# Routing of a two-layer PEER trunk: index of head 0 first, four early gathers behind it, half 6 of the query weights split by VectorE

## What is computed

```python
q = (xt @ w_q).reshape(n_tok, PEER_HEADS, 2, D_QHALF)          # 8 heads, two halves of 128 each
sc = einsum("thcd,hckd->thck", q, sub_keys)                    # scores against 128 keys per half
top_s, top_i = top_k(sc, 16)                                   # "keys"
cand_s = top_s[:, :, 0, :, None] + top_s[:, :, 1, None, :]
best_s, best_j = top_k(cand_s, 16)                             # "pairs"
experts = take_along_axis(top_i0 * 128 + top_i1, best_j)       # "part": the index
gates = softmax(best_s)
h = einsum("thkd,td->thk", u_tab[experts], x)                  # 128 rows of 8 KB per token
out = einsum("thk,thkd->td", gates * gelu(h), v_tab[experts])
```

## Time and profile before

| | |
|---|---|
| median of 3 executions | 3293.93 us (3290.31 to 3294.55) |
| profiled execution: its time | 3297.1 us |
| profiled execution: span from first to last instruction | 3295.4 us |
| mean granted TensorE clock | 0.943 of 2.4 GHz |
| query product of layer 0 | 358.9 to about 461.2 us |
| query product of layer 1 | about 2043 to 2146 us |
| first ring dots (`first_dots`) of layer 0, layer 1 | 466.4 us, 2150.6 us |

### The profile page before, as it was taken

How to read it: one execution, slowest core, us unless ns; L and a number is a source line. 1 busy time by engine, 2 the same in 40 slices (tenths; PEclk the granted TensorE clock), 3 DMA queues, 4 the chain that set the end, 5 groups by cost and what they waited for, 6 DMA issues and landing times.

```text
span 3295.4 us, 44606 instructions
## 1 busy us (share of the span) xinstructions
PE 2879.7 (87%) x15107; PEld 2210.8 (67%) x15107; DVE 2466.0 (75%) x3641; ACT 825.6 (25%) x1274; POOL 1557.6 (47%) x1313
## 2 busy tenths in 40 slices
PE   9999987667777899999899999977768777999998
PEld 8887887666777644444697977966667776444443
DVE  6996698999999766666533555898899988766666
ACT  1014432113433500000233534422224335200000
POOL 0000567767677644444200002777676777544443
PEclk9999998888988999999999999988789889999999
DMA  8434499999999899999765334799999999999998
GB/s 259 153 128 153 150 362 422 421 421 412 419 417 421 309 410 406 409 409 402 267 211 179 129 138 156 258 409 421 422 422 416 416 419 353 376 410 405 409 407 344
DMA packets 293996, 1108.20 MB, mean 336 GB/s; under 512 B 22068, under 2 KB 120948, under 8 KB 220788
## 3 DMA queue, kind: packets, MB, share of 16 engines
q0 software_dynamic: 147456, 805.37, 60.3%
q1 hardware_dynamic: 146420, 301.26, 25.3%
HBM read 1104.45 MB, written 2.10 MB: 336 GB/s over the span
## 4 chain that ended last, share of the span: by engine, by line
DMA 39%; PE 27%; DVE 15%; issue 9%; POOL 7%; ACT 2%; SPq 0%; POOLq 0%; DVEq 0%; ACTq 0%
DMA ring<-in_peer_u,index_now 17%; DMA work<-in_peer_v,index_add 13%; PE ps L865 6%; DMA more_add<-in_peer_v,index_add 6%; PE ps L762 5%; DVE ring L1870 5%; POOL ring L604 5%; PE ps L805 5%; DVE ps L1942 3%; PE ps L816 2%; DMA work<-in_peer_v,index_v 2%; PE ps L944 1%; PE ps L1048 1%; DMA ring<-in_peer_w_q 1%; PE ps L1026 1%
## 5 line engine op out<-in xcount | busy, mean ns | idle before, releaser
L604 POOL DMA_INDIRECT ring<-in_peer_u,index_now x480 | 793.0, 1652 | 343.9 <-issue 137.9
L1870 DVE SCALAR_TENSOR_TENSOR ring<-ring,x_tok 128x2048 f32<-128x2048 f32 x372 | 843.4, 2289 | 102.8 <-DMA ring<-in_peer_u,index_now 101.5
L1101 PE MATMUL ps<-all_v,mix 128*128 128x512 f32 x1984 | 851.8, 592 | 0.0
L1101 PEld LDWEIGHTS ps<-all_v,mix 128*128 128x128 f32 x1984 | 377.0, 190 | 474.5 <-issue 474.5
L1054 PE MATMUL ps<-x_dot,work 128*128 128x128 f32 x3968 | 524.9, 296 | 113.3 <-DVE ps L1877 73.1
L1942 DVE SCALAR_TENSOR_TENSOR ps<-work,coef,ps 128x1024 f32<-128x1024 f32 x326 | 419.0, 1288 | 244.9 <-DMA work<-in_peer_v,index_add 202.6
L1054 PEld LDWEIGHTS ps<-x_dot,work 128*128 128x128 f32 x3968 | 502.4, 209 | 142.9 <-ACT work L1404 72.2
L588 POOL TENSOR_TENSOR w_lo<-ring,w_hi 128x512 fp32r<-128x512 f32 x104 | 134.0, 1324 | 829.2 <-ACT w_hi L1234 804.9
L1404 ACT ACTIVATE work<-ps 128x1024 f32<-128x1024 f32 x248 | 243.6, 1022 | 611.2 <-PE ps L1048 610.7
L1632 DVE TENSOR_TENSOR w_lo<-ring,w_hi 128x2048 fp32r<-128x2048 f32 x85 | 194.8, 2292 | 246.9 <-ACT w_hi L1234 246.8
L714 POOL DMA_INDIRECT work<-in_peer_v,index_add x256 | 242.0, 945 | 268.2 <-DVE ps L1942 220.5
(11 more groups left out here) (234 smaller groups left out, 3811.9 us busy)
## 6 DMA issues: line engine op xcount, KB each, us to landing
all_v<-in_peer_v SPq DMA_DIRECT2D x248, 512.0 KB, 6.8
ring<-in_peer_w_q SPq DMA_DIRECT2D x16, 2048.0 KB, 9.4
ring<-in_attn_w_kv SPq DMA_DIRECT2D x16, 2048.0 KB, 8.7
ring<-in_conv_w_in SPq DMA_DIRECT2D x14, 2048.0 KB, 9.0
ring<-in_conv_w_out SPq DMA_DIRECT2D x8, 2048.0 KB, 7.4
ring<-in_attn_w_q SPq DMA_DIRECT2D x8, 2048.0 KB, 8.2
ring<-in_attn_w_o SPq DMA_DIRECT2D x8, 2048.0 KB, 7.3
ring<-in_peer_u,index_now POOLq DMA_INDIRECT x480, 13.7
```

The costliest lines, as they stand in the source:

```text
L604: pool.indirect_dma_start(tile, None, u_tab, bass.IndirectOffsetOnAxis(ap=index_now[:, half, s:s + 1], axis=0)).then_inc(landed_in, 16)
L1101: mm = pe.matmul(ps[:, dense_bank(tb, q), :], mix[tb][:, row, :], tile[:, q * 512 - HALF:(q + 1) * 512 - HALF], start=False, stop=True, sk ...
L1870: dve.scalar_tensor_tensor(out=tile, in0=tile, scalar=1.0, in1=x_tok[:, tb, :], op0=ALU.mult, op1=ALU.mult, accum_out=coef[:, tb, slot]).t ...
```

## The change

The same operations on the same data are done in another order, with four differences of substance.
1. The index is made for head 0 alone (a part of 1 head), then for heads 1 to 3 together (3 heads). Before, heads 0 and 1 were indexed together, and then heads 2 and 3. The third part (heads 4 to 7) stays.
2. GpSimd splits halves 0 to 5, issues e0 to e3 in one go, and then splits half 7. VectorE splits half 6. From half 8 on they take turns as before. The gathers e4, e5 and e6, e7 stand at other places between the halves.
3. VectorE's dots of early tiles stand as 3, 3 and 2 between other work (2, 1, 2, 2 and 1 before); `route_keys` of token block 1 moves behind the keys and pairs of heads 4 and 5.
4. ScalarE places x into PSUM after half 2 instead of after half 1.

```diff
-                for u in range(8):
+                for u in range(6):
                     split_half(U_WQ[layer] + u)
                 pool.wait_ge(route[layer], part_done(0, 0))
-                gather_early(0, 3)
+                gather_early(0, ROOMS)
+                next_half(7)
+                gather_early(ROOMS, ROOMS + 1)
                 next_half(9)
-                gather_early(3, 5)
+                gather_early(ROOMS + 1, ROOMS + 3)
                 next_half(11)
-                gather_early(5, 7)
+                gather_early(ROOMS + 3, EARLY)
                 next_half(13)
-                gather_early(7, EARLY)
...
                 gather_first(4, U_RING)
+                pool.wait_ge(route[layer], part_done(0, 1))
                 for group in (2, 3):
...
-                for tb, first, group, pairs in ((0, 2, 4, 2), (0, 4, 8, 4), (1, 0, 0, 4), (1, 4, 8, 4)):
+                for tb, first, group, pairs in ((0, 1, 4, 2), (0, 4, 8, 4), (1, 0, 0, 4), (1, 4, 8, 4)):
...
                     if m == 1:
                         take_keys()
+                    if m == 2:
                         act.wait_ge(sk_taken, 4 * (layer + 1))
...
-                for h in range(2):
-                    route_keys(layer, 0, h, h + 1)
-                    route_pairs(layer, 0, h, h + 1)
-                part_numbers(layer, 0, 0, 2)
+                route_keys(layer, 0, 0, 1)
+                route_pairs(layer, 0, 0, 1)
+                part_numbers(layer, 0, 0, 1)
                 for c in range(2):
-                    part_key(layer, 0, 0, 2, c)
-                part_index(layer, 0, 0, 2)
+                    part_key(layer, 0, 0, 1, c)
+                part_index(layer, 0, 0, 1)
+                route_keys(layer, 0, 1, 2)
+                next_half(6)
+                route_pairs(layer, 0, 1, 2)
+                early_dots(0, 3)
                 next_half(8)
-                route_keys(layer, 1, 0, 2)
-                early_dots(0, 2)
+                early_dots(3, 6)
+                route_keys(layer, 0, 2, 4)
                 next_half(10)
-                route_keys(layer, 0, 2, 4)
-                early_dots(2, 3)
+                early_dots(6, EARLY)
                 route_pairs(layer, 0, 2, 4)
                 next_half(12)
-                early_dots(3, 5)
+                part_numbers(layer, 0, 1, 4)
+                for c in range(2):
+                    part_key(layer, 0, 1, 4, c)
+                part_index(layer, 0, 1, 4)
+                next_half(14)
                 route_keys(layer, 0, 4, 6)
-                next_half(14)
-                early_dots(5, 7)
                 route_pairs(layer, 0, 4, 6)
-                early_dots(7, EARLY)
-                part_numbers(layer, 0, 2, 4)
-                for c in range(2):
-                    part_key(layer, 0, 2, 4, c)
-                part_index(layer, 0, 2, 4)
+                route_keys(layer, 1, 0, 2)
                 first_dots(0, U_RING // 2)
```

More of the change, by code:

```diff
@@ L47 @@
 LN_HEAD = 9
-ROUTING = (("keys", 0, 0, 1), ("pairs", 0, 0, 1), ("keys", 0, 1, 2), ("pairs", 0, 1, 2), ("part", 0, 0, 2),
-           ("keys", 1, 0, 2), ("keys", 0, 2, 4), ("pairs", 0, 2, 4), ("keys", 0, 4, 6), ("pairs", 0, 4, 6), ("part", 0, 2, 4),
+ROUTING = (("keys", 0, 0, 1), ("pairs", 0, 0, 1), ("part", 0, 0, 1), ("keys", 0, 1, 2), ("pairs", 0, 1, 2),
+           ("keys", 0, 2, 4), ("pairs", 0, 2, 4), ("part", 0, 1, 4), ("keys", 0, 4, 6), ("pairs", 0, 4, 6), ("keys", 1, 0, 2),
            ("keys", 0, 6, 8), ("pairs", 0, 6, 8), ("logits", 0, 0, 8), ("part", 0, 4, 8), ("gate", 0, 0, 8),
```

## The result

The changed kernel takes 3343.55 us (median of 4, 3342.79 to 3344.54) against 3293.01 us of the kernel before: ratio 1.0157, interval 1.0145 to 1.0170. It is 50.5 us slower. The forecast was slower, 3328 us, with a range up to 3338: the direction was right and the size was too small, by 15.5 us. The profiled execution took 3344.5 us with a span of 3342.8 us.

A forecast was written before the change was run, and what follows sets the result against it. TensorE paces the query product and DMA bytes bound the dot phase behind it. Two TensorE stalls per layer delay the ring dots 17 us, twice 17 = 34 us on 3293.9 gives 3328 us; range 3308 to 3338.

The forecast's parts named there:

- The pace of the product and the bound behind it: TensorE paces the query product, waiting about 0.6 us in 13; the dot phase behind is bound by bytes at 422 GB/s.
- Step 1: Half 9 is rounded at 409.03 us as before, split by GpSimd from 411.50 to 416.5; e5's gather issues at 416.68.
- The weighing of the two queues: Gather beside a panel: half of 422 GB/s gives 7 us to landing; the measured row, 8.7 us, was used instead.
- Steps 2 and 3: e5 lands after 8.7 us at 425.4; VectorE idles some 9 us, splits half 10 at 435.2; TensorE stalls 7.3 us.
- Steps 4 and 5: e7 lands at 448.9, half 12 is split at 456.7; TensorE stalls 9.0 us, the product is 15.8 us late.
- Step 6: VectorE's three-head part takes 11 us ahead of half 14, split at 469.9; the product ends 16.5 us later.
- Step 7: VectorE reaches the first ring dot at 483.8 us, 17.4 us later than before; 17 us taken per layer.
- The clock: TensorE slow after stalls: up to 3 us per layer, 3334 to 3340 us, left out of the middle value; chance 0.08.
- Tiles that are there in time: Rival: e5 and e7 landed when VectorE needs them, e5 by 418 us; no change, 3294 us, chance 0.07.
- a gain: Rival: the filled DMA hole at 390 us brings panels and ring tiles earlier; at most 7.5 us per layer, chance 0.07.

The follow-up runs named there:

- e0: Not a run: the first of the eight early gathers of `u` in a layer, a tile of 1 MB; the forecast had it issued at 391 to 392 us.
- b: Changed kernel with only two early gathers ahead of half 7, the next three behind it: 3328.93 us, ratio 1.0117 to the kernel before.
- c: Changed kernel with two gathers ahead of half 7, dots of e4, e5 behind half 10 and of e6, e7 behind half 12: 3297.18 us, ratio 1.0023.
- k: Kernel before with the index of head 0 made first and alone, heads 1 to 3 together later, splits and gathers in place: 3291.94 us, ratio 1.0006.

## Why the prediction was right in direction and too small

**The pace of the product and the bound behind it** held. TensorE's product paced the stretch before, the phase behind it moved 422 GB/s in both kernels, and a lateness at the first ring dots was still there at the end (46.0 us there, 47.4 us in the span).

**Step 1 failed.** It said that half 9 is rounded at 409.03 and that "this doesn't move". It moved by 6.8 us to 415.83, and its split from 411.50 to 418.12. I had asked when the gathers could be issued, and had taken the hole in the DMA stream as free; I had not asked what else was being loaded in that hole. Panel 4 was: released at 391.5 us by the split of half 5, which also lets GpSimd go on to the gathers (it stood 0.61 us more, for the index). With four of them beside it, and e4 behind, it took 22.2 us where it had taken 9.4. ScalarE wanted it at about 403 and got it at 413.7; TensorE's slack up to half 8 was used up and 5.2 us on top. The rows for this were at hand: the panels beside gathers had taken 13.9 to 16.5 us in the kernel before, one of them in the earlier trace rows. The forecast added no term for a panel at all.

**The weighing of the two queues** was wrong with it. From the page "DMA: Bandwidth & Descriptors" of the Trainium skill (Queues, rings and completion order) I took that the DMA engines take turns between the queues packet by packet, and made "half of 422 GB/s" of it. Turns by packet are not turns by byte: with packets of 7.3 and 1.0 KB equal turns give the gathers 88% of the bytes, and from 399 to 411 us the trace shows just that, 594 and 589 packets and 4.34 of 4.93 MB. The page's packet is a group of descriptors, and that it is what the profile counts as a packet, no run shows; by the profile's packets the turns are one for one, and the rule speaks against this change. What the runs show is that panel 4 lands late with the gathers beside it and in time with fewer of them (b); packets of another size were not tried.

**Steps 2 and 3** held, 6.5 us late. e5 was issued at 423.30 and landed 8.5 us later (8.7 forecast), VectorE stood 9.4 us (some 9), and the half was split at 441.6 instead of 435.2. The stall of TensorE was 7.2 us (7.3).

**Steps 4 and 5** held. From one split to the next it took 441.6 to 463.2, 21.6 us (21.5 forecast). The stall was 6.9 us and not 9.0, because TensorE came out of the stall before at its slow clock and needed 14.6 us for its own work instead of 12.5; the moment at which half 12 was split didn't depend on that, as the forecast said.

**Step 6** was 0.9 us short: the part of three heads took 463.16 to 475.06, 11.9 us (11).

**Step 7** came out at 491.3 us instead of 483.8. Of these 7.5 us, 6.6 are step 1 and 0.9 the part. Twice 7.5 and the 34 of the forecast are 49 us; 50.5 were measured. Layer 0 lost 25.1 us and layer 1 25.9 where the forecast had 17 for each.

**The clock** was a bound of the range, "up to 3 us per layer". After the two long stalls the 16 products of a `w_lo` pass took 3.78 and 3.68 us instead of 2.08, and the granted clock was 0.62 and 0.61 of 2.4 GHz in the stretches of 438 to 444 and 462 to 468 us, the mean of a part at 1.2 GHz (0.5) and a part at 2.4 GHz (1). Three stalls of 5.2 + 7.2 + 6.9 = 19.3 us made the product end 24.2 us late (last copy of a half at 485.37 against 461.21); about 5 us are slow matmuls. The ring dots were 25.1 us late by VectorE's own list, in which none of the slow products stands. So in layer 0 the clock does not add to them, as forecast. Whether the ring gathers that wait for the end of the product would have held the phase up by themselves, no run shows.

**The rivals.** Tiles that are there in time, and a gain, did not come about. Their condition, e5 landed by 418 us, failed by 14 us. That the early gathers, which I had given up to 7.5 us per layer, gain nothing was tried by c, with two of them at 391.5 us, and by k.

## What to carry to other kernels

A transfer asked for earlier into a half-empty DMA stream is not free: look up what is loaded there now, who waits for it, and how large the packets of both are. When the earlier request and a load that is on the path are released at nearly the same moment, the load can be the one that pays, as the one with the smaller packets did here. In a list that an engine works off in order, a consumer of a transfer must not stand ahead of work that the request for it waits on indirectly; follow each wait once around the loop over all engines, and write down what stands between it and the next thing that another engine needs.

## What the runs showed of the hardware

Gathers of 8 KB rows hold a load with 1 KB pieces back far more than the other way round: 22.2 us against 9.4 for a panel of 2 MB, while a gather beside a panel took 8.5 us and alone 5.7 (a gather of the changed kernel at 468.6 us). A gather's instruction on GpSimd takes 0.94 us, but 3.02 us (e2's, begun at 394.76 us) where it fell together with VectorE's split (394.68 to 396.9 us), and 2.93 us in the same situation in the kernel before. Small operations of VectorE took 1.2 us beside GpSimd's subtractions (1.26 us each), against 0.2 without them. The page "SBUF — State Buffer" of the Trainium skill (SBUF: two separate sides) says that the two engines share a pair of ports, which one instruction holds to its end while the other engine waits; on VectorE's side this holds for an instruction in a mode of two ports, or with two inputs in SBUF while GpSimd's reads SBUF. The trace agrees: the first and the last of these rows have two inputs in SBUF, and all four end when GpSimd's do. In which mode the two between ran, the trace does not say.

```profile
463.46 1.21 DVE L1781 SCALAR_TENSOR_TENSOR row_f<-row_j 128x48 f32<-128x48 uint32 x1
464.59 1.32 DVE L1783 CAST work<-work 128x96 f32<-128x96 uint32 x1
465.95 1.18 DVE L1785 TENSOR_SCALAR row_f<-row_f 128x48 f32<-128x48 f32 x1
467.17 1.24 DVE L1788 SCALAR_TENSOR_TENSOR row_f<-row_f 128x48 f32<-128x48 f32 x1
```

They end at 464.67, 465.91, 467.13 and 468.41 us, 1.24 to 1.28 us apart, and GpSimd's split of half 13 ran from 463.32 to 468.34 in four instructions, 1.26 us each.
